# The fourth weight sum of the seven-product jobs: from an adding transfer to VectorE

## The reference, cut to what matters

```
def swiglu(h, wg, wu, wd):
    return (jax.nn.silu(h @ wg) * (h @ wu)) @ wd
xs = xs + gt2 * swiglu(modulate(rmsnorm(xs, g_ffn[l]), sh2, sc2), w_gate[l], w_up[l], w_down[l])
```

## Time and profile before

| | |
|---|---|
| median of three runs | 889.78 us |
| time of the profiled execution | 892.12 us |
| its span, first to last instruction | 890.3 us |
| TensorE busy in it | 878.0 us (99%) |
| VectorE busy | 705.7 us (79%) |
| ScalarE busy | 467.8 us (53%) |
| software queue of GpSimd's transfers | 41.11 MB, 24.3% of the 16 engines' span |
| mean granted clock of TensorE | 0.996 of full speed |

### The profile page before, as it was taken

The page is one execution under the profiler, slowest core; times in us unless marked ns, Lnnn a source line. Parts: engine busy times, 40 slices in busy tenths (PEclk is TensorE's granted clock), DMA queues, the critical chain, the costliest instruction groups (busy, mean ns, idle before and its releaser), DMA issues. The chain is left out here.

```text
span 890.3 us, 16552 instructions
## 1 busy us (share of the span) xinstructions
PE 878.0 (99%) x6235; PEld 835.3 (94%) x6235; DVE 705.7 (79%) x1330; ACT 467.8 (53%) x973; POOL 122.3 (14%) x155
## 2 busy tenths in 40 slices
PE   7999999999999999999999999999999999999997
PEld 5789888898989999999999999999999999999997
DVE  5467899799788599874777869997687998777987
ACT  5574444777777533442246645555454555544553
POOL 0000000010000000000000033313323322333221
PEclk8999999999999999999999999999999999999999
DMA  9954344441443220237307289878999886898866
GB/s 367 365 194 165 141 143 139 150 127 63 157 154 118 72 69 3 76 115 318 131 24 237 64 186 200 177 173 191 196 202 196 190 188 165 193 211 183 186 154 143
DMA packets 51663, 145.32 MB, mean 163 GB/s; under 512 B 6000, under 2 KB 12416, under 8 KB 50176
## 3 DMA queue, kind: packets, MB, share of 16 engines
q1 hardware_dynamic: 32000, 102.38, 34.7%
q0 software_dynamic: 18864, 41.11, 24.3%
q10 hardware_dynamic: 720, 0.77, 0.2%
HBM read 121.68 MB, written 12.20 MB: 150 GB/s over the span
## 5 line engine op out<-in xcount | busy, mean ns | idle before, releaser
L1320 ACT ACTIVATE w_hi<-stage 128x512 fp32r<-128x512 f32 (+1 forms) x186 | 106.3, 608 | 94.9 <-DMA stage<-stage 49.1
L2013 DVE TENSOR_TENSOR w_lo<-stage,w_hi 128x512 fp32r<-128x512 f32 (+1 forms) x186 | 117.9, 667 | 26.2 <-ACT w_hi L1320 25.9
L2632 PE MATMUL ps<-m_hi,w_lo 128*128 128x320 f32 x304 | 93.9, 309 | 0.0
L2632 PE MATMUL ps<-m_lo,w_hi 128*128 128x320 f32 x304 | 93.9, 309 | 0.0
L2632 PE MATMUL ps<-m_hi,w_hi 128*128 128x320 f32 x304 | 93.9, 309 | 0.0
L2632 PE MATMUL ps<-h_hi,w_hi 128*128 128x320 f32 x272 | 84.1, 309 | 1.6 <-DVE w_lo L2013 1.6
L1415 DVE TENSOR_TENSOR w_lo<-stage,w_hi 128x1024 fp32r<-128x1024 f32 x47 | 57.3, 1222 | 35.8 <-ACT w_hi L887 35.5
L2632 PE MATMUL ps<-h_hi,w_lo 128*128 128x320 f32 x272 | 84.0, 309 | 0.0
L2632 PE MATMUL ps<-h_lo,w_hi 128*128 128x320 f32 x272 | 84.0, 309 | 0.0
L2632 PE MATMUL ps<-y_hi,w_hi 128*128 128x320 f32 x264 | 81.7, 309 | 0.0
L2632 PE MATMUL ps<-y_hi,w_lo 128*128 128x320 f32 x264 | 81.6, 309 | 0.0
(11 more groups left out here) (319 smaller groups left out, 2443.1 us busy)
## 6 DMA issues: line engine op xcount, KB each, us to landing
stage<-w_main SPq DMA_DIRECT2D x118, 512.0 KB, 4.2
x<-w_ada SPq DMA_DIRECT2D x21, 512.0 KB, 4.6
stage<-stage POOLq DMA_DIRECT2D x38, 256.0 KB, 4.5
qk<-w_ada SPq DMA_DIRECT2D x7, 1024.0 KB, 13.2
scr<-w_main POOLq DMA_DIRECT2D x28, 256.0 KB, 6.2
y_t<-scr POOLq DMA_DIRECT2D x22, 320.0 KB, 7.1
s_second<-w_main POOLq DMA_DIRECT2D x26, 256.0 KB, 6.4
stage<-w_main POOLq DMA_DIRECT2D x19, 256.0 KB, 6.8
```

Source lines behind the costliest of these rows:

```text
L1320: act.activation(w_hi[:, slot, at:at + job_half(j) * P], left_stage(op, j), ACT.Copy).then_inc(left_hi[op], 1)
L2013: dve.tensor_tensor(w_lo[:, slot, w], left_stage(op, j), w_hi[:, slot, w].bitcast(F32), ALU.subtract).then_inc(left_lo[op], 1)
L2632: ins = pe.matmul(ps[:, BANK_OF[op], 0:TH], wt[:, slot, w], right(op, part, j, k), start=k == 0 and n == 0, stop=k == half - 1 and n == 2)
```

## The change

For the 20 jobs that had GpSimd's adding transfer, VectorE makes S4 with the function it already has. For job 0 this stands ahead of `y_sums_low(1)`; for job j+1 it stands in the loop of job j, behind the low part of S2(j+1) and ahead of `c22_u3(j)`. The 11 jobs of which VectorE made it before keep their place (behind the low part of A12(j+1)). The transfer `s4` and its two calls leave GpSimd's queue, its semaphore `s4_sum` is gone, and ScalarE's high part of S4 waits on VectorE's semaphore; ScalarE's own order is not changed.

```diff
         def sum_made(op, j):
             if op == "S3":
                 return s3_sum, 16 * (j + 1)
+            if op == "S4":
+                return s4_own, N_SEVEN + j + 1
             n = sum_number(j)
             if sums_by_vector(j):
-                return {"S1": s1_own, "S2": s2_own, "S4": s4_own}[op], N_SEVEN + n
-            return {"S1": s1_sum, "S2": s2_sum, "S4": s4_sum}[op], 16 * n
+                return {"S1": s1_own, "S2": s2_own}[op], N_SEVEN + n
+            return {"S1": s1_sum, "S2": s2_sum}[op], 16 * n
...
-            def s4(j):
-
-                pool.wait_ge(*sum_made("S2", j))
-                pool.wait_ge(left_lo["A12"], nth(j))
-                pool.dma_start(left_stage("S4", j), left_stage("S2", j), accum_op=ALU.add).then_inc(s4_sum, 16)
-
...
             s2(0)
             s3_second_term(0)
-            s4(0)
             s1(1)
...
-                if by_transfers(j + 1):
-                    s4(j + 1)
                 if j + 2 < len(JOBS):
                     s3_second_term(j + 2)
...
             left_low("S1", 0)
             left_low("S2", 0)
+            s4(0)
             y_sums_low(1)
             left_low("A22", 0)
...
                 else:
                     last_tile(0, high_sb, slice(0, T)).then_inc(last_done, 1)
+                if more and not own_sums:
+                    s4(j + 1)
                 c22_u3(j)
```

More of the change, by code:

```diff
@@ L461, in hybrid_dit_program @@
         left_hi, left_lo, left_used = ({op: sem(f"{kind}_{op}") for op in LEFT} for kind in ("hi", "lo", "used"))
-        s1_sum, s2_sum, s3_sum, s4_sum = (sem(f"s{i}_sum") for i in (1, 2, 3, 4))
+        s1_sum, s2_sum, s3_sum = (sem(f"s{i}_sum") for i in (1, 2, 3))
         s3_in = sem("s3_in")
```

## The result

The change makes the kernel slower. Medians of 15 runs each: 894.21 us (890.24 to 896.03) after, 890.49 us (888.67 to 892.08) before; ratio 1.0036 with a 95% interval of 1.0026 to 1.0047, so 2.3 to 4.2 us. The forecast was 889.5 us in 887.8 to 891.4. Of the rivals B, which wanted 892.2 us, comes nearest; how far its mechanism holds is told behind the experiments.

The account below looks back on a forecast made before the run. TensorE, busy 99% of the span, was taken as the bound: 892.12 - 1.87 (stop gone) + 1.6 (new stops) = 891.85, carried to the runs' median as 889.78 - 0.27 = 889.5 us; range 887.8 to 891.4.

Parts of the forecast that it names:

- B: Rival: SP's earlier load collides with S2's transfer in light jobs, first down jobs stop about 1.4 us; 892.2 us, chance 0.13.
- The stop at S4(1), 1.87 us, goes: Job 1: TensorE's wait for S4(1)'s low part vanishes because VectorE makes S4(1) earlier; win 1.87 us, lower end 1.5.
- 0.60 us for an add; 12.18 becomes 12.78 us in a wide job; 11.41 becomes 11.88 in job 26: VectorE gets 0.60 us more in each of 20 jobs; in 640-wide jobs its lag behind TensorE (12.32) grows by 0.46.
- Light jobs hide it: Tile jobs of a part's first half: the add fits VectorE's idle time behind `left_low`, 2.17 us in job 1.
- No issue of S2 is held while VectorE works: GpSimd's S2 issues: the shared-port rule would delay one by up to 0.69 us; the rows show none, none priced.
- Where a lag reaches TensorE, lag - 1.52 + 0.08 at jobs 5 and 17: Lag: from the next job's first matmul to `c21`'s start; at 2.0 jobs 5 and 17 stand 0.56 us each.
- Only the first down job of each part needs what VectorE made just before: Jobs 5, 17 and 27 were taken as the only places where VectorE's lag can make TensorE stand.
- I take a lag of 0.6 at the start of jobs 2, 14 and 25: VectorE's lag entering the wide jobs, 0.6 us, near most light jobs' 0.2 rather than 1.5 after slow transfers.
- the earlier load against the freed queue: S2's transfer: S4's transfer leaving the queue helps, SP's earlier 512 KB load beside it hurts; median landing 5.2 us taken.
- The same step in parts 1 and 2: Lag of 0.6 us at jobs 14 and 25, giving stops of 0.56 us at job 17 and 0.5 at job 27.
- The sum: Lags of 2.0 at jobs 5 and 17, stops together 1.6 us against the 1.87 us win, net -0.27 us.
- S2(1) lands at 525: Sum S2(1) lands at 525 instead of 526.8, since S4(0)'s transfer no longer holds up the issues behind it.

Follow-up runs that it names:

- e4: Changed kernel with the 20 new adds cut to 32 of their 512 (384) columns; ratio to the kernel before 0.9993, stage 369.53 us.
- e5: Changed kernel with each of its 20 new adds made twice, one behind the other; ratio to the kernel before 1.0182, stage 389.93 us.
- e2: Changed kernel, but jobs 3, 4, 5, 15, 16, 17, 26 and 27 keep GpSimd's adding transfer, so no add in a wide job; ratio to before 0.9993.
- e7: Changed kernel with SP's load of A11 and A12 of job j+2 held back until c11(j) is made; ratio to the kernel before 0.9998.
- e6: Changed kernel with the add of S4(j) moved behind times_up(j-1) in job j, ahead of S3(j)'s low part; ratio to the kernel before 1.0004.
- e9: Changed kernel with both edits of e6 and e7 (add moved, SP's load held back); median 889.41 us, ratio to the kernel before 0.9976.
- e8: Changed kernel, but VectorE makes S4 by the new add in job 1 only, the other 19 jobs keep the transfer; ratio to before 0.9979.
- e10: Kernel before with one edit: SP's load waits for c11(j), GpSimd still makes all 20 S4 sums; median 889.67 us, ratio to before 0.9983.
- e1: Changed kernel, but VectorE makes S4 by the new add in jobs 0 and 1 only, the other 18 keep the transfer; ratio to before 0.9993.
- e3: Changed kernel, but only jobs 3, 4, 5, 15, 16, 17, 26 and 27 have the new add, the others keep the transfer; ratio to before 1.0024.

## Why the prediction was wrong, point by point

- *The stop at S4(1), 1.87 us, goes*: right, in after and in every kernel with S4(1) by VectorE.
- *0.60 us for an add; 12.18 becomes 12.78 us in a wide job; 11.41 becomes 11.88 in job 26*: right (12.78, and 11.98 in job 26, 0.1 more), and e4 and e5 show that it is the instruction's time.
- *Light jobs hide it*: right (e2).
- *No issue of S2 is held while VectorE works*: right, they took 865 to 901 ns in after.
- *Where a lag reaches TensorE, lag - 1.52 + 0.08 at jobs 5 and 17*: right in place, low in size at job 5. With a lag of 3.02 it should have stood 1.6 and stood 1.9: `times_up` started 0.46 us after the end of `c21`, where 0.11 is usual, which no rule of mine had; it did so in job 5 of e4 and e7 too. Its cause stays open. Job 17 with 2.55 should have stood 1.1 and did. "Only the first down job of each part needs what VectorE made just before" was wrong: I had left out the stops for S4's low part in jobs 3 and 4, 0.5 us, which come from a lag of about 2.6 on.
- *"I take a lag of 0.6 at the start of jobs 2, 14 and 25"*: this step failed, at job 2 above all, where the lag was 2.16. I set it near "the 0.2 of most light jobs", but only jobs 0 and 1 stand ahead of job 2, and S2(1) is the sum that took longest to land of all (7.8 us). My own terms would have given more: S2(1) at 525 puts `c21(0)` at 527.8, 1.4 us behind the start of job 1 (526.35 before), and one light job of 11.8 us takes off 0.5, so 0.9. Measured, S2(1) came 1.0 us later than that in the times of before, which made the lag 2.47 at job 1, and job 1 took VectorE 12.01 us, as S2(2) took 5.4 us to landing and not 3.8. e7 shows that this is S2's landing: with S2(1) at 5.2 us and S2(2) at 3.4 the lag at job 2 is 0.20. I weighed the earlier load against the freed queue as if the two cancelled; in the median they did (5.3 us against 5.2), but not for S2(2).
- *The same step in parts 1 and 2*: at jobs 14 and 25 the lag was the least, 0.20. Jobs 14 and 15 then added 0.63 and 0.34 more than the add. The first is S2(15)'s landing, and most of it stood in the trace of before, where job 14 took VectorE 12.74 us, 0.56 more than the other wide jobs. The second is no landing but the idle 0.46 us ahead of `c12(15)`, which is also there in e4, e6, e7 and e9, with S2(16) at 3.4 us in two of them; its cause stays open. In job 27 the stop that I had at 0.5 us was 0.1 more than before, because job 25 began with 0.20.
- *The sum*: with 2.16 and 0.20 + 0.97 in place of 0.6 the same working gives 3.5 and 2.6 at jobs 5 and 17 where I had 2.0 and 2.0; the stops on the way take 0.5 off the first. Against the forecast job 5 stood 1.4 us longer, jobs 3 and 4 0.5, job 17 0.5 and job 27 0.4 less: 2.0 us, which takes the forecast's -0.27 to the measured +1.8. The two idle times have 0.7 of it.
- *S2(1) lands at 525*: 525.7, and it had to be before 523.7 to leave no lag.

What rival B named, the load beside S2's transfer, is shown by e7 to slow that transfer. As a forecast B was right in direction and in job 5 (it had a lag of 1.5 at job 2, measured 2.16), but not elsewhere: it had 1.5 at jobs 14 and 25 too, where the lag was 0.20, a stop of 1.4 us in job 27, where 0.1 was lost, and landings of 6 us, where the median is 5.3. It had 0.13, too little.

What stays open is the size of the whole: the profiled stages differ by 1.8 us, the medians by 3.7. Three things outside the stage are on record. The tail is 0.7 us longer in after's profile. The time beyond the span is 2.1 us in after's runs and 1.8 in those of before (medians), 0.3 us more. And the two profiled executions differ in TensorE's clock near their start. The windows 16 to 20 and 20 to 24 us, first before, then after (the number ahead of the last two is the granted clock):

```profile
16.00:20.00 4.00, 4.00 (x26) 3.31 (x29) 2.29 (x5) 1.10 (x3) 0.65 (x1) 0.50 1.02 418
20.00:24.00 4.00, 4.00 (x33) 1.96 (x26) 2.03 (x3) 2.76 (x6) 0.00 (x0) 0.73 1.01 409
```

```profile
16.00:20.00 4.00, 4.00 (x38) 2.97 (x34) 1.66 (x3) 0.38 (x1) 0.65 (x1) 0.67 1.00 412
20.00:24.00 4.00, 3.83 (x37) 2.02 (x27) 3.38 (x7) 3.97 (x8) 0.00 (x0) 1.00 1.03 418
```

In e2, e8, e9 and e10 both windows have 1.00, and the stage begins at 512.1 to 512.7 us. In e1, e4, e5 and e6 only the first is lower, as in after, and the stage begins at 513.3 to 514.2. In e3 and e7 both are lower, as in before, and it begins at 514.4 to 514.9. So a part of the scatter from run to run arises ahead of everything that the change touches. In the 35 runs of before beside e1 to e4 the 12 with a mean clock of 1.000 took 890.0 us in the median and the 7 with 0.996 or less 892.1. The profiled execution of before took 892.12, with 0.996, well above its median, so the profiles show less of the loss than the medians. That landings differ between executions (e1 and e2 above) adds to the scatter; how much isn't shown.

## What to carry to other kernels

On an engine whose period is within 0.2 us of the bound's, an added instruction is hidden only where the engine idles: price it as its length times the jobs in a row without slack, and look for who needs the result at the end of that row. Take the lag at the start of that row from the jobs that stand ahead of it, not from an average. When a stop comes from a late transfer, look first for what runs beside that transfer; here one held-back load did what 20 adds were to do. The adds cost TensorE nothing in the jobs with slack (e2), and in the others nearly nothing when they stood where the engine idled and the load was held back (e9). And where several stops of a microsecond are exchanged, compare the stage in the profiles beside the medians, and the granted clock ahead of it.

## What was unexpected

Behind the stops of 2.0 and 2.5 us in e5 TensorE's granted clock fell from 1.00 to a mean of 0.57, and its matmuls show the lower of the two levels, 1.2 GHz: 0.27 us apart instead of 0.147, 12 of them in job 17. There it fell 1.8 us after TensorE had started again, in job 27 at once. The stop of 1.6 us in after and those of 1.8 and 1.1 us in other runs were not followed by it. In job 17 of e5 the lower clock took about 12 x 0.12 = 1.5 us more, which is part of what e5 lost beyond its forecast. TensorE's timeline of e5:

```profile
742.25 0.47 PE L2631 MATMUL ps<-y_lo,w_hi 128*128 128x320 f32 x1
742.52 0.47 PE L2631 MATMUL ps<-y_hi,w_lo 128*128 128x320 f32 x1
742.79 0.47 PE L2631 MATMUL ps<-y_hi,w_hi 128*128 128x320 f32 x1
```

In e5's job 5 a stop of the same 2.0 us was not followed by a lower clock, so the length of the one stop does not decide it alone.
